# Low keys times high queries as two 64-row products, first layer by pairs of heads, bias in three parts

## The reference

```
layer 0, 16 heads of 64:  s = q.k * scale + bias[head, row offset, column offset]   # keys: 8 x 16 window round the query
                          s_ctx = q.k_ctx * scale                                   # and all 256 context keys
                          y = softmax([s, s_ctx]) . [v window, v_ctx]
                          (the 256 context queries attend to the context keys alone)
layer 1, 8 heads:         for each of two maps m, 64 dims each: p[m] = softmax(q[m].k[m] * scale)   # all 1280 keys
                          y = rms_norm((p[0] - lambda * p[1]) . v)
both:                     h = x * (1 + scale) + shift;  q, k, v, z = split(h @ w_in)
                          x = layer_norm(alpha * x + (1 + g) * ((y * silu(z)) @ w_out))
```

## Time and profile before

| | |
|---|---|
| median of 3 runs | 2119.4 us |
| the profiled execution | 2119.15 us, span 2117.3 us |
| PE busy | 1913.3 us, 90% |
| DVE (VectorE) busy | 1297.0 us, 61% |
| ACT (ScalarE) busy | 890.6 us, 42% |
| mean granted clock of PE | 0.965 |
| scores of layer 1, L1367 | 768 matmuls, 192.3 us |
| scores of layer 0, L1051 and L1055 | 320 and 256 matmuls, 77.2 and 66.8 us |

### The profile page before, as it was taken

The page is one execution under the profiler, slowest core; times in us unless marked ns, Lnnn a source line. Parts: engine busy times, 40 slices in busy tenths (PEclk is TensorE's granted clock), DMA queues, the critical chain, the costliest instruction groups (busy, mean ns, idle before and its releaser), DMA issues. The chain is left out here.

```text
span 2117.3 us, 31607 instructions
## 1 busy us (share of the span) xinstructions
PE 1913.3 (90%) x11121; PEld 1629.3 (77%) x11121; DVE 1297.0 (61%) x2074; ACT 890.6 (42%) x1560; POOL 148.0 (7%) x155
## 2 busy tenths in 40 slices
PE   6879799999999999968989999999999989998697
PEld 2768687978888888856867878787887878787576
DVE  1557384747474757585875566565747474747567
ACT  0434253535354444451134536463636363635410
POOL 4234000000000000001100000000000000000000
PEclk9899899999999999998999999999999999999899
DMA  8476422222222222125411010101000000001142
GB/s 272 67 59 49 110 62 55 62 54 64 58 61 56 63 54 65 44 91 179 149 70 40 11 40 10 40 10 38 12 30 20 30 20 23 16 20 40 55 175 100
DMA packets 137392, 130.80 MB, mean 62 GB/s; under 512 B 46672, under 2 KB 112560, under 8 KB 137216
## 3 DMA queue, kind: packets, MB, share of 16 engines
q1 hardware_dynamic: 125008, 98.22, 16.3%
q0 software_dynamic: 9744, 22.51, 6.0%
q10 hardware_dynamic: 2592, 9.44, 1.1%
HBM read 110.81 MB, written 22.00 MB: 63 GB/s over the span
## 5 line engine op out<-in xcount | busy, mean ns | idle before, releaser
L528 PE MATMUL acc<-h_hi,w_hi 128*128 128x512 f32 (+1 forms) x1408 | 524.7, 373 | 14.6 <-DVE w_lo L497 5.0
L528 PE MATMUL acc<-h_lo,w_hi 128*128 128x512 f32 (+1 forms) x1408 | 512.4, 364 | 0.0
L528 PE MATMUL acc<-h_hi,w_lo 128*128 128x512 f32 (+1 forms) x1408 | 512.3, 364 | 0.0
L528 PEld LDWEIGHTS acc<-h_hi,w_hi 128*128 128x128 f32 x1408 | 269.4, 191 | 55.6 <-issue 15.8
L528 PEld LDWEIGHTS acc<-h_hi,w_lo 128*128 128x128 f32 x1408 | 268.6, 191 | 42.4
L528 PEld LDWEIGHTS acc<-h_lo,w_hi 128*128 128x128 f32 x1408 | 269.6, 191 | 33.6
L1367 PE MATMUL acc<-k_dup,q_stack 128*128 128x512 f32 (+1 forms) x768 | 192.3, 393 | 38.2 <-DVE q_stack L709 24.5
L1281 DVE TENSOR_REDUCE stats<-acc 128x1 f32<-128x1280 f32 x128 | 190.3, 1487 | 53.0 <-PE acc L1367 52.9
L940 ACT ACTIVATE pt<-acc 128x256 f32<-128x256 f32 (+1 forms) x288 | 123.4, 432 | 203.5 <-PE acc L1065 203.3
L1367 PEld LDWEIGHTS acc<-k_dup,q_stack 128*128 128x128 f32 x768 | 145.9, 205 | 79.6 <-issue 24.4
L1388 PE MATMUL acc<-pt,v 128*128 128x128 f32 x1280 | 175.0, 277 | 0.8
(11 more groups left out here) (189 smaller groups left out, 2725.1 us busy)
## 6 DMA issues: line engine op xcount, KB each, us to landing
w_raw<-in_w_in SPq DMA_DIRECT2D x64, 512.0 KB, 4.1
extra_prob<-in_w_mod SPq DMA_DIRECT2D x40, 256.0 KB, 2.8
w_raw<-y_t POOLq DMA_DIRECT2D x18, 512.0 KB, 5.6
w_raw<-in_w_out SPq DMA_DIRECT2D x16, 512.0 KB, 3.3
big<-in_w_mod SPq DMA_DIRECT2D x24, 256.0 KB, 2.8
y_t<-y SPq DMA_DIRECT2D x8, 640.0 KB, 3.4
y_t<-y SPq DMA_DIRECT2D x8, 512.0 KB, 2.8
big<-x POOLq DMA_DIRECT2D x8, 512.0 KB, 3.7
```

The source lines that it names most:

```text
L528: mm = nc.tensor.matmul(m.bank(self.bank_of(j), w), wt[:, b % 2, k, :], ht[:, k, t0:t0 + w], start=(k == 0 and i == 0), stop=(k == KT - 1 ...
```

## The change

It has four parts.

1. `k_dup` becomes `k_hi` (both halves, as part 0 before) and `k_lo` (one array, head 0's low keys in partitions 0 to 63, head 1's in 64 to 127). The second product of the scores is a 64-row one on the head's own partitions: q_hi.k_lo. The term q_lo.k_lo is no longer computed. ScalarE copies only k_hi.
2. Layer 1: for each tile, the six 64-row products of the two maps are issued together, alternating between the maps (and so between the halves of the partitions), after both maps' 128-row products.
3. Layer 0: items alternate between the heads; one step is a pair of items of the same tile. Scores of a pair wait for both exponentials of the pair before. Transposes and values of a pair come one step later. Fillings are laid anew: none of the next chunk's in pair 7. `gate_y` takes two tiles of both heads, in two instructions.
4. The bias is loaded, and waited for, in three parts, by the kind of window (left edge, inner, right edge): 16 DMAs each, first used by pairs 0, 2 and 6, reloaded after pairs 2, 6 and 8.

```diff
@@ layer 1, PE @@
-                    def scores(mp, t):
+                    def first_scores(mp, t):
                         if t:
                             pe.wait_ge(exp_done, CREDIT + c * 2 * NQ + (2 * (t - 1) + mp + 1))
                         for g, (k0, w) in enumerate(GROUPS):
-                            for part in range(2):
-                                mm = nc.tensor.matmul(m.bank(3 * mp + g, w), m.q_stack[:, mp, t * P:(t + 1) * P],
-                                                      m.k_dup[:, mp, part, k0:k0 + w], start=(part == 0), stop=(part == 1))
-                        mm.then_inc(s_done, 1)
+                            nc.tensor.matmul(m.bank(3 * mp + g, w), m.q_stack[:, mp, t * P:(t + 1) * P],
+                                             m.k_hi[:, mp, k0:k0 + w], start=True, stop=False)
+
+                    def second_scores(t):
+                        for g, (k0, w) in enumerate(GROUPS):
+                            for mp in range(2):
+                                own = slice(64 * mp, 64 * mp + 64)
+                                mm = nc.tensor.matmul(m.bank(3 * mp + g, w), m.q_stack[own, mp, t * P:(t + 1) * P],
+                                                      m.k_lo[own, k0:k0 + w], start=False, stop=True)
+                                if g == 2:
+                                    mm.then_inc(s_done, 1)
...
                         if t + 2 < NQ:
-                            scores(1, t + 2)
+                            first_scores(1, t + 2)
+                            second_scores(t + 2)
@@ layer 0 @@
-    items = [Item(h, n) for h in range(2) for n in range(TOK_TILES)]
+    items = [Item(h, n) for n in range(TOK_TILES) for h in range(2)]
...
+    fill = {(0, END): (0, z1, 0, 8), (1, MIDDLE): (0, z2, 0, 4), (1, END): (0, z2, 4, 8),
+            (6, MIDDLE): (1, 2, 0, 4), (6, END): (1, 2, 4, 8)}
+    for step in range(2):
+        for half in range(2):
+            k = 4 * step + 2 * half
+            fill[2 + step, half] = (1, 0, k, k + 2)
+            fill[4 + step, half] = (1, 1, k, k + 2)
+            fill[8 + step, half] = (1, 3, k, k + 2)
@@ layer 0, ScalarE @@
+                    for step in range(PAIRS + 1):
+                        old = of_pair[step - 1] if step else []
+                        for n in old[:2]:
+                            evac(n)
+                        if step < PAIRS:
+                            exp(2 * step)
+                        for n in old[2:3]:
+                            evac(n)
+                        if step < PAIRS:
+                            exp(2 * step + 1)
+                        for n in old[3:]:
+                            evac(n)
+                        take_filled(step)
@@ layer 0, VectorE @@
+                    for step in range(PAIRS):
+                        if step in first_pair:
+                            kind = first_pair.index(step)
+                            v.wait_ge(bias_loaded[kind], CREDIT + c * BL[kind] + BL[kind])
+                        row_max(2 * step)
+                        if step % 2 and step >= 3:
+                            gate_y(step // 2 - 1)
+                        row_max(2 * step + 1)
+                        normalise(2 * step)
+                        normalise(2 * step + 1)
+                        if step in filled and not filled[step][0]:
+                            p.gate_silu(v, c, filled[step][1])
+                        if 1 <= step <= KT:
+                            late.sum(v, c, step - 1)
@@ layer 0, PE @@
+                    def scores(q):
+                        if q:
+                            pe.wait_ge(exp_done, CREDIT + c * NI + 2 * q)
+                        pair = [(2 * q + h, items[2 * q + h]) for h in range(2)]
+                        for i, it in pair:
+                            lhs, k = it.queries(m.q_stack[:, it.head, :]), m.k_hi[:, it.head, :]
+                            if it.local:
+                                nc.tensor.matmul(local_scores(i), lhs, it.keys(k), start=True, stop=False)
+                            nc.tensor.matmul(ctx_scores(i), lhs, k[:, SEQ:TOK], start=True, stop=False)
+                        if pair[0][1].local:
+                            for i, it in pair:
+                                nc.tensor.matmul(local_scores(i), it.queries(m.q_stack[it.rows(), it.head, :]),
+                                                 it.keys(m.k_lo[it.rows(), :]), start=False, stop=True)
+                        for i, it in pair:
+                            nc.tensor.matmul(ctx_scores(i), it.queries(m.q_stack[it.rows(), it.head, :]),
+                                             m.k_lo[it.rows(), SEQ:TOK], start=False, stop=True).then_inc(s_done, 1)
...
+                    for step in range(PAIRS + 1):
+                        if step < PAIRS:
+                            scores(step)
+                        for position, n in enumerate(of_pair[step - 1] if step else []):
+                            turn(n)
+                            if n >= 2:
+                                values(n - 2)
+                            if position == 1:
+                                fill_in(step, MIDDLE)
+                        fill_in(step, END)
```

More of the change, by code:

```diff
@@ L70 @@
 CREDIT = 1
+AHEAD = 4
 ROW_PAD = P
-AHEAD = 4
 def f(ap):
@@ L284, in bias_parts @@
 def bias_parts():
-    parts = []
+    parts = [[] for kind in range(KINDS)]
     for b in range(ROW_BLOCKS):
@@ L297, in bias_parts @@
                     at = kind * K_STRIPS + low - K_STRIP0[(0, 1, COL_BLOCKS - 1)[kind]]
-                    parts.append((half * 64 + s * CELL, b, at, high - low + 1, first - K_BAND0[b], last - first + 1,
-                                  rows, cols * NEAR + low - strip + 1, first - band + 1))
+                    parts[kind].append((half * 64 + s * CELL, b, at, high - low + 1, first - K_BAND0[b], last - first + 1,
+                                        rows, cols * NEAR + low - strip + 1, first - band + 1))
     return parts
@@ L551, in pe_part @@
         if self.NV > 3:
-            self.product(pe, c, AHEAD + 1)
+            first += 1
+            self.product(pe, c, first)
         self.turn_v(pe, c, self.NV - 1)
-        for j in range(AHEAD + (2 if self.NV > 3 else 1), self.cum[2]):
+        for j in range(first + 1, self.cum[2]):
             self.product(pe, c, j)
[L556 to L559, removed]
+        gate_bank_free(pe)
+        self.product(pe, c, self.cum[2])
         pe.wait_ge(self.q_ready, CREDIT + (c + 1) * 2 * self.q_groups)
         pe.wait_ge(self.k_ready, CREDIT + c * 2 + 2)
[L563 to L571, removed]
+        pe.wait_ge(self.k_own, CREDIT + c * 2 + 2)
     def evacuate(self, act, c, j):
@@ L783, in queries, with rows @@
         return q[:, pos * P:(pos + 1) * P]
+    def rows(self):
+        return slice(64 * self.head, 64 * self.head + 64)
     def keys(self, k):
@@ L801, in neighbourhood @@
     bias_set = stack.enter_context(nc.semaphore("n_bias_set"))
-    bias_loaded = sem("bias_loaded")
+    bias_loaded = [sem(f"bias_loaded{kind}") for kind in range(KINDS)]
     s_done, biased, max_done = sem("s_done"), sem("biased"), sem("max_done")
@@ L895, in _ @@
                 sp.wait_ge(bias_set, 1)
-                for h in range(2):
-                    load_bias(biases[0], 0, h)
+                for kind in range(KINDS):
+                    load_bias(biases[0], 0, kind)
                 each_chunk(sp, chunk)
@@ new lines, in chunk @@
+                    p.dve_part(v, c, last)
+                    for step in range(PAIRS):
[12 more added lines that the diff above has]
+                            late.sum(v, c, step - 1)
+                        if step == 3 and not last:
+                            p.split_lo_part(v, c, 5)
+                        if 2 <= step < 2 + KT and last:
+                            out_w.split_lo(v, step - 2)
@@ L1123, in _ @@
+                    if last:
+                        pe.wait_ge(p.gate_done, CREDIT + c * p.q_groups + 3)
+                    else:
+                        pe.wait_ge(p.evac, CREDIT + (c + 1) * p.cum[2] + 3)
+                    late.reduce(pe, c)
+                    values(NT - 2)
+                    values(NT - 1)
                 each_chunk(pe, chunk)
@@ L1398, in chunk @@
                     p.pe_part(pe, c, lambda e: e.wait_ge(y_ready, CREDIT + c * 2))
-                    scores(0, 0)
-                    scores(1, 0)
-                    p.late_product(pe, c)
-                    scores(0, 1)
-                    scores(1, 1)
-                    p.before_turns(pe, c)
+                    first_scores(0, 0)
+                    first_scores(1, 0)
+                    second_scores(0)
+                    p.product(pe, c, p.G - 1)
+                    first_scores(0, 1)
+                    first_scores(1, 1)
+                    second_scores(1)
+                    pe.wait_ge(p.gate_done, CREDIT + c * p.q_groups + 1)
```

(2 more changed lines are left out.)

221 lines of the change are left out of this document (75 added, 146 removed).

## The result

Four runs of the changed kernel took 2205.91 us in the median (2201.58 to 2210.9), beside 2119.56 for the kernel before on the same chip (2115.71 to 2120.5). The ratio is 1.0412 (95% interval 1.0386 to 1.0437). The prediction was 2196 us, range 2155 to 2238. The profiled execution took 2206.27 us, its span is 2204.5 us.

What follows compares the result with a forecast made beforehand. PE was taken to bound both layers. Layer 1 +88, layer 0's chunks 1 to 6 -14 and its last chunk +3 made +77 on 2119.15: 2196 us, range 2155 to 2238.

Steps and rivals of the forecast that it cites:

- The joined ring: Layer 1: both maps' score rings become one, map 0's maximum waiting for map 1's previous exponential; 7.94 us against 5.87.
- the slack of 0.64: Layer 1, transposes of tile 6: they start 0.64 us after their operand is there, taken off each chunk's growth.
- The last chunk: Layer 1's last chunk: its own stall of 3.57 us exceeds the new wait of 2.98, so only +2.0.
- Overlap: Layer 1: paired 64-row products run at once, a tile's second products costing 0.635 us instead of 1.27.
- rival 1: Both layers: the halves do not overlap; 2238 us, or 2220 with changes of shape at nothing; chance 0.17.
- the change of shape: PE, both layers: switching between whole and 64-row products; 0.15 us lost per layer 1 round, 20 changes per layer 0 chunk.
- The clock: Layer 1's ring: a quarter of the time at 1.2 GHz, five rounds paying +1.2 us per chunk.
- rival 3: Layer 1's ring: PE's part always at 1.2 GHz, 45 us instead of 8; 2233 us; chance 0.08.
- Layer 0's middle chunks: PE covers the pair's ring except at pair 7; idle 3.9 us becomes 1.5, -2.4 per chunk, -14 over chunks 1 to 6.
- the 0 that I gave the halves: Layer 0, per chunk: 2.9 us saved with overlap less 20 changes of shape, between +3 and -2.9, taken as 0.
- The bias in three parts: Layer 0: removes a wait before chunk 0's first scores, but that gain is given back; value 0.
- the later anchor: Layer 0: chunk 1's scores start at 254.06 behind the store of y, which follows the bias table, whatever PE does.

Runs made afterwards that it cites:

- e5: The kernel before with the changed kernel's order of layer 1's scores but whole 128-row second products; 2224.19 us, ratio 1.0505.
- e1: The changed kernel with only layer 1's scores as before, the new layer 0 kept; 2112.35 us, ratio 0.9976.
- e6: e1 with whole 128-row second products in layer 0 as well; 2106.63 us, ratio 0.9938.
- e4: The changed kernel, layer 1 reordered: VectorE's two maxima ahead of the combination, PE's next scores ahead of the transposes, evacuations moved to match; 2169.8 us, ratio 1.024.
- e7: e1 with SyncE storing the row and y ahead of the third bias part's load; 2106.94 us, ratio 0.9947.
- e8: e7 with the second bias part's load moved behind the store too; 2108.9 us, ratio 0.9945.
- e3: The kernel before with 64-row second products in layer 1, each map's behind its own first ones with its own s_done; 2163.6 us, ratio 1.0217.

## Why the prediction was right

**The joined ring** was the forecast's main term, and it holds in mechanism and size. I gave 7.94 us with overlap plus 0.15 for the shape; measured 8.13. VectorE's 4.96 and the 1.51 to PE's first matmul came out the same (1534.10 + 1.48 = 1535.58 to 1537.08 is 1.50), and PE's part is 1.66 (1537.08 to 1538.74) where I had 1.47 + 0.15. Chunks were to be 12.3 longer; the six middle ones are 12.4. e5 shows that it is the order that costs, e1 that the rest of the change does not. That the chunk comes out so near is in part luck. In the chunk of the earlier trace rows the six rounds take 48.23 us (1400.87 to 1449.10) where my terms give 46.96 + 0.9 + 1.2 = 49.06, and the slack of 0.64 behind them, which I took off, did not go off: the rest of the chunk takes 74.17, before 73.87. The two misses cancel.

**The last chunk** was put at +2.0 and is +3.9. In that chunk both kernels have rounds of about 8.54 us, set by the split of w_out, as I had said. Only the first round grows, from 4.47 (1931.05 to 1935.52) to 7.43 (2014.61 to 2022.04), by 3.0, and two of the later ones are 8.72 and 8.73. The prediction gives 2.0 for the first round without a working; its own figures for that round, 3.49 and 6.47, give 2.98, and nothing of this was absorbed.

**Overlap** was right, and rival 1 is out: 0.78 us for six halves, in pairs that start 1 to 10 ns apart. What I undersized is the change of shape: 0.15 us, where each costs 0.19. In the ring this is hardly seen (1.66 for 1.62), since of the second change, behind the halves, 0.11 falls on the values, which the maximum does not wait for; in layer 0, with twenty changes a chunk, it is. The Trainium skill, "TensorE: Matmul & The Clock Gate", Part 3, has packed products at up to 3.07 times the speed for four tiles; here two tiles are 1.5 times as fast in their own 0.78 us (1.16 / 0.78), and with all that the two changes cost the gain is 0.17 us of 1.16.

**The clock** (my 1.2 us per chunk, rival 3 for more) stayed near the small value: over the whole span it is 0.958 against 0.965. I had spread the slow quarter over five rounds; it falls on the first. That round is 7.16 us (1400.87 to 1408.03) for my 6.47, at a granted clock of 0.76, while those after it are 8.12 to 8.14 at 1.00, but for one of 8.55 with the weight split (forecast 8.73). In the next chunk the first round is 7.36 at 0.77, and the last one too is slow, 8.81 at 0.81; so that chunk takes 123.28 us and not 122.40.

```profile
1400.87:1408.03 7.16, 4.72 (x21) 3.42 (x21) 3.48 (x4) 3.92 (x6) 0.00 (x0) 0.76 0.00 0
```

**Layer 0's middle chunks**: -2.4 forecast, -2.1 measured (104.0 to 101.9), and the gap at pair 7 is there with 1.42 of the 1.5 forecast (0.64 before 415.68 and 0.78 before 418.05). But the 0 that I gave the halves is a loss of 0.9 us per chunk (e6), so the order itself gives 3.0. The sum came out because the two misses are of opposite sign.

**Layer 0's first chunks** were off. I gave -2.4 to six chunks; five have it. Up to the store of chunk 1 the change is behind by 2.8 us (333.53 against 330.74), because everything up to there hangs on the bias table, which was finished at 218.97 instead of 216.41, and chunk 1 does not get its 2.4. From its first scores to its store it takes 76.61 us (256.92 to 333.53), before 76.68. A part of this is the clock: behind the longer idle time the granted clock is 0.50 to 261 and 0.68 from there to 265; in the kernel before it is 0.50 to 258 and 0.95 from there to 262. Layer 0's last chunk is +4.2 for the +3 forecast. Together layer 0 is -3.65 in the profiled execution where I had -11. With 90.5 for the +88 of layer 1 the two misses explain the 10 us between 2196 and 2206. How layer 0's part divides is less sure than layer 1's: with the same layer 0 the last store comes at 943.39 in e1 and 940.74 in e4 (945.72 here), which is 6.0 and 8.6 us earlier than in the kernel before, and the last chunk is +2.6 and +3.2.

**The bias in three parts** gave nothing that can be seen, as forecast, and for the reason that I gave: chunk 1's scores started at 256.92 (254 forecast; the table was 2.6 us later), behind an idle time of 17.20. No run takes this part out alone; e7, which moves the third part behind the store, builds on it. One sentence of the forecast was wrong. I wrote that the change removes a wait before the first scores of chunk 0. The wait stands behind the first scores, and 8.79 us of its 11.98 stay: VectorE stands 13.13 us for a split of weights, whose load is queued on SyncE behind the 48 bias loads (40.07 us of issue from 88.67). I had not followed the queue past those loads. It cost nothing, only because the later anchor takes it up.

```profile
140.01 0.69 PE L1044 MATMUL acc<-k_hi,q_stack 128*128 128x384 f32 x1 [8.79 <-ACT big L921]
```

## What to carry to other kernels

When products of two independent loops are put side by side, look first at what their common signal ties together: here a gain of 0.17 us of matmul time per tile joined two rings into one and cost 2.3. Halves of the array pay only in long runs: a run of 64-row products between whole ones must save more than two changes of shape, 0.38 us here. By this price, as an estimate, more than 0.76 us of whole products must be replaced at once; measured are a loss at 0.58 (layer 0) and a gain at 1.16 (layer 1), nothing between them. A gain ahead of a fixed anchor (here a store behind 48 loads on one queue) is worth nothing until the anchor is moved, and then the order on the queue alone gave 5.4 us (e1 to e7). Moving sixteen loads more (e8) brought nothing on top, since the next weights then wait behind them.

## What was unexpected of the hardware

A 64-row matmul with nothing on the other half is no faster than a whole one: in e3 a map's three halves take 0.78 us and its three whole products 0.76, each with a part of a change in it. Each change between 128-row and 64-row products costs some 0.19 us in the stream (half of 0.37), and the weight load that otherwise runs ahead stands 0.25 us there. Pairs on the two halves do run fully side by side, with fp32r operands and both adding to banks that whole products had begun: six take the 0.78 us of three.
